# Routing by token block through a table in memory, and a slot of one row tile ahead of the widest expert's slot

## The chip, the cores and the metric

The kernel runs on one core of a Trainium2 chip. The metric is the device time of one execution in microseconds, as the median of several runs. The core has four compute engines that matter here: TensorE (PE, matrix products and transposes; PEld is its weight load), VectorE (DVE), ScalarE (ACT) and GpSimd (POOL). SyncE (SP) issues most of the transfers; GpSimd issues the indirect ones, which gather or scatter rows by a list of indices.

## The reference, cut to what matters

One decoder layer on 1024 tokens of width 1024, all in float32: a mixer (attention and a state-space branch), a cross attention to 256 memory tokens, a mixture of 32 experts with 4 of them per token, and a final norm. The change touches the seam between the cross attention and the experts:

```
h = h + cross_attention(rmsnorm(h), rmsnorm(mem))        # last step: o @ w_o, added to h
xn = rmsnorm(h, norm_moe)
logits = xn @ w_router + b_router                        # (1024, 32)
top_val, top_idx = top_k(logits, 4)
gates = softmax(top_val)
# every expert e gets the list of its tokens, in the order of the tokens:
hb = xn[tokens of e] @ w1[e] + b1[e]                     # 1024 -> 2048
act = clamped swiglu(hb)
h[tokens of e] += gate * (act @ w2[e] + b2[e])           # 1024 -> 1024
out = rmsnorm(h, norm_final)
```

## The kernel before

The kernel has two phases. The first, `phase_abc`, isn't touched. The second, `phase_def`, runs `mixer`, `router` and `experts` one behind the other on each engine's own instruction stream; semaphores order the engines among each other.

**mixer** ends with the output product of the cross attention, the group `XO`: for 8 blocks of 128 tokens and 2 halves of 512 columns, 4 products accumulate in one PSUM bank (the emitting line for all such products is L1247, a helper). VectorE adds each half to `h` (L1353), ScalarE squares and sums `h` (L1493), and GpSimd takes the root (L297 to L299). `moe_row` (L1133) multiplies a block of `h` by its root and by the gain row `g_row` into `xn` or `xnb`, four quarter products a block. Four of the eight blocks are made among the additions and four behind them.

**router** works on all 1024 tokens at once, stage behind stage. SP stores `h` to `acc_dram` (L1559, L1560) and `xn` to `xn_dram` (L1563). TensorE transposes `xn` (L1593), ScalarE and VectorE copy it out as `hT` (L1579, L1634), TensorE makes the logits with the router weights stationary and 512 tokens moving (L1601), and transposes them back (L1607). VectorE finds the top 8 per token (L1649, L1653), makes one-hot rows for the four chosen experts (`m4`, L1662) and their sum `maskE` (L1665). Two products with a triangle and with ones (L1612, L1613) give the rank of each token in its expert's list. VectorE sums counts over blocks (L1675), ranks the experts by their load (L1679 to L1686, result `slot_e`; with this SP asks for the first 12 weight pieces, L1573) and splits the rank into a low part of 7 bits and a high part (L1694 to L1699). The lists come from one-hot products: for 32 pairs of a block and a choice, VectorE makes `lo`, `hi` with the token and `hi` with the gate (L1707 to L1709) and TensorE multiplies them into one bank (L1616). From this bank come the token list, the gate list and, by another product (L1620), the indices of quarter rows `idx_q` (L1719).

**experts** works through slots. `RANK_WIDTH` gives each rank in the order of load a width of rows, from 256 for the fullest expert down to 64 for the two emptiest, which share a slot. `SLOTS` is the order of the slots: rank 0 (256 rows) first, the pair (30, 31), then ranks 1, 29, 2, 28 and so on, and at last 16, 15 and 14 with 128 rows each. The weights of an expert are 12 pieces of 1 MB (8 of w1, 4 of w2) in a ring of 14 places; `load_piece` (L1789) on SP waits until the piece that held the place has been used (`piece_used`). A slot goes so: GpSimd copies the slot's indices (`columns`, L2009 to L2014), gathers quarter rows of `xn_dram` (L2023, four gathers for each tile of 128 rows, 32 tokens by 4 quarters each), VectorE transposes them (L2328) into `xT`, TensorE makes the first layer (L2224, 256 instructions), VectorE and ScalarE the activation, TensorE the second layer: by columns for slots wider than 128 (L2239), by rows for slots of up to 128 (L2147, behind a bias product L2179). GpSimd scatters the result by adding to `acc_dram` (L2042). VectorE clears some tiles at the start of this stage (L2310 to L2317); the semaphore `init_f` counts them, and SP, TensorE and GpSimd wait for its eight steps before their first expert work. Behind the last slot `fin` is read back, normed and stored.

Of the kernel before, what the change touches and what calls it, by code (L numbers as in the profile page):

```python
# [16 lines left out]
F32 = mybir.dt.float32  # L17
# [32 lines left out]
SLOTS = ((0,), (30, 31)) + tuple((r,) for i in range(1, 14) for r in (i, 30 - i)) + ((16,), (15,), (14,))  # L50
# [47 lines left out]
def memory(nc, ctx):  # L98
# [110 lines left out]
    at("br", 201.9375, [E, 1])  # L209
    at("logitT", 194, [E, S])  # L210
    at("logit", 162, [P, NB, E])
    at("top8", 163.5, [P, NB, 8])
    at("idx8", 164, [P, NB, 8], U32)
    at("idxf", 164.5, [P, NB, 8])
    at("gates", 165, [P, NB, 8])
    at("gsum", 165.5, [P, 2, NB])
    at("m4", 165.75, [P, NB, TOPK, E])
    at("maskE", 170, [P, NB, E])
    at("rank", 171, [P, NB, E])
    at("pref", 172, [P, NB + 1, E])  # L220
    at("tri", 173.5, [P, P])
    at("iota_e", 174, [P, E])
    at("iota_w", 174.5, [P, WIN])
    at("dest", 175.5, [P, 4, NB * TOPK])
    at("desti", 176.25, [P, 2, NB * TOPK], I32)
    at("tok1", 176.75, [P, NB])
    at("dumpid", 177, [P, WIN])
    at("lo", 178, [P, 4, P])
    at("hi", 180, [P, 4, 2, WIN])
    at("list_f", 198, [P, 2, WIN])  # L230
    at("list_t", 200, [P, 2, WIN])
# [7 lines left out]
    at("idx_g", 49, [P, WIN], I32)  # L239
# [24 lines left out]
    at("g_row", 0, [P, D])  # L264
# [861 lines left out]
def moe_row(nc, m, b):  # L1126
# [4 lines left out]
    for q in range(4):  # L1131
        out = (m.xn, m.xnb)[b // 4][:, b % 4, WIN * q:WIN * q + WIN].rearrange("p (k r) -> p k r", r=32)
        last = nc.vector.scalar_tensor_tensor(out=out, in0=part(m.h[:, b], q), scalar=m.rs[:, b:b + 1], in1=part(m.g_row[:], q), op0=ALU.mult, op1=ALU.mult)  # L1133
# [3 lines left out]
def mixer(nc, m, a, sem, xn3, g_row_in):  # L1137
# [37 lines left out]
    plan("XO", 16, "dve")  # L1175

# [34 lines left out]
    def on_sync(sp):  # L1211
# [18 lines left out]
        sp.wait_ge(filled, at["XQ"] + 8)  # L1230
        sp.dma_start(m.g_row[:], a.norm_moe.rearrange("(a n) -> a n", a=1).to_broadcast([P, D])).then_inc(g_row_in, 16)

    def on_tensor(pe):
# [98 lines left out]
        copied(pe, at[("O", 7)])  # L1332
        pe.wait_ge(wxo_in, 16)
        for b in range(NB):
            for n in range(2):
                product(lambda k: m.oT[:, k, b * P:(b + 1) * P], lambda k: m.wxo[:, k, n * 512:(n + 1) * 512], 512, H_X)

    def on_vector(dve):
# [91 lines left out]
        copied(dve, index("PB", 15))  # L1430
# [1259 lines left out]
```

## Time and profile before

| | us |
|---|---|
| median of 3 runs | 2451.79 |
| lowest and highest run | 2443.67 and 2454.3 |
| the profiled execution, its own time | 2438.7 |
| its span, first to last instruction | 2437.0 |
| output product of the cross attention starts | 718.2 |
| first expert product starts | 877.1 |
| mean granted TensorE clock | 0.978 |

| engine | busy us | share of the span |
|---|---|---|
| TensorE | 2297.0 | 94% |
| VectorE | 675.6 | 28% |
| ScalarE | 302.6 | 12% |
| GpSimd | 542.3 | 22% |

The profile is one execution. Times in a timeline count from the span's start. A row of a timeline merges equal instructions of one line (x128 is their number) and gives when the first began and how long the whole took. The text in brackets is the idle time of the engine ahead of it and what ended it; "issue" is time in which the engine waited for nothing that the profile shows. Shares of busy time are averages over stages with different limits, so the stages have to be read one by one.

### The profile page before, as it was taken

Reading aid. Unit: us, or ns where it says so; the run is one execution under the profiler, and the core shown is the slowest. Engines: PE = TensorE matmul, PEld = TensorE weight load, DVE = VectorE, ACT = ScalarE, POOL = GpSimd, SP = SyncE. Lnnn points to the kernel's source line nnn. Section 1 sums busy time; section 2 is a strip of 40 time slices with the busy share of each in tenths; the row PEclk is TensorE's granted clock in tenths of the full one; section 3 lists DMA queues with packets and bytes.
Section 4 is the critical chain, followed back from the end, with each engine's and each line's share of the span. In section 5 each row is a group of like instructions: output and inputs, shape, how many; then the busy total and the mean of one; then the engine's idle time right before and its main releaser. Section 6 shows DMA issues by size and latency. Waiting matters only on the chain.

```text
span 2437.0 us, 33822 instructions
## 1 busy us (share of the span) xinstructions
PE 2297.0 (94%) x13692; PEld 1765.9 (72%) x13693; DVE 675.6 (28%) x1684; ACT 302.6 (12%) x637; POOL 542.3 (22%) x1123
## 2 busy tenths in 40 slices
PE   7999988989979669999999999999999999999997
PEld 4546545534444257698988989889889899899875
DVE  2131247223154722122222222212222222222213
ACT  3002045112032000000000010000000100100002
POOL 3715885011002030202011120111111211211203
PEclk9999999999999879999999999999999999999998
DMA  8614210720002645988688798888988989989985
GB/s 202 133 46 48 55 30 2 209 87 0 7 3 117 245 142 186 366 286 286 224 278 298 251 300 265 291 281 265 299 285 271 307 282 312 310 294 305 318 301 165
DMA packets 441043, 508.81 MB, mean 209 GB/s; under 512 B 50997, under 2 KB 367765, under 8 KB 440884
## 3 DMA queue, kind: packets, MB, share of 16 engines
q1 hardware_dynamic: 426968, 470.42, 58.9%
q0 software_dynamic: 12624, 35.90, 6.1%
q8 instruction: 109, 1.79, 0.3%
q10 hardware_dynamic: 1292, 0.30, 0.1%
q14 instruction: 50, 0.41, 0.0%
HBM read 470.60 MB, written 38.25 MB: 209 GB/s over the span
## 4 chain that ended last, share of the span: by engine, by line
PE 76%; DVE 3%; issue 1%; ACT 1%; POOL 1%; ACTq 0%; POOLq 0%; DVEq 0%
PE ps L2224 40%; PE ps L2239 11%; PE ps L1247 10%; PE ps L2147 10%; PE ps L1616 1%; PE ps L2126 1%; PE ps L2179 1%; ACT px L1474 1%; PE ps L1261 1%; PE ps L1601 1%; DVE px L1408 0%; DVE negx L1398 0%; POOL rs L298 0%; DVE xnb L1133 0%; PE ps L1254 0%
## 5 line engine op out<-in xcount | busy, mean ns | idle before, releaser
L2224 PE MATMUL ps<-xT,we 128*128 128x128 f32 (+10 forms) x7680 | 981.6, 290 | 23.8 <-issue 23.8
L2224 PEld LDWEIGHTS ps<-xT,we 128*128 128x128 f32 x7680 | 970.1, 191 | 39.2 <-issue 31.9
L2363 DVE TENSOR_SCALAR glu<-ps,b1s 128x128 f32<-128x128 f32 (+10 forms) x240 | 88.9, 370 | 963.9 <-PE ps L2224 951.6
L2239 PE MATMUL ps<-actT,we 128*128 128x160 f32 (+9 forms) x1792 | 261.1, 307 | 0.0
L2023 POOL DMA_INDIRECT xg<-xn_dram,gx x148 | 152.7, 1031 | 474.1 <-DVE xT L2328 434.4
L2239 PEld LDWEIGHTS ps<-actT,we 128*128 128x128 f32 x1792 | 253.8, 190 | 5.6 <-DVE outT L2389 2.0
L2147 PE MATMUL ps<-we,actT 128*128 128x512 f32 (+1 forms) x576 | 238.2, 595 | 0.7 <-ACT actT L2538 0.7
L2514 ACT ACTIVATE sg<-glu 128x256 f32<-128x256 f32 (+10 forms) x122 | 55.0, 451 | 1253.4 <-DVE glu L2363 1196.7
L2042 POOL DMA_INDIRECT acc_dram<-orow,sx x43 | 66.9, 1556 | 605.0 <-ACT orow L2502 426.5
L2147 PEld LDWEIGHTS ps<-we,actT 128*128 128x128 f32 (+1 forms) x576 | 100.4, 184 | 136.6 <-issue 135.7
L806 PE MATMUL ps<-xnT,wa 128*128 128x512 f32 x384 | 167.9, 598 | 7.1 <-DMA wa<-in_w_in 7.1
L806 PEld LDWEIGHTS ps<-xnT,wa 128*128 128x128 f32 x384 | 73.4, 192 | 99.2 <-issue 91.3
L2389 DVE TENSOR_SCALAR outT<-ps,b2s 128x160 f32<-128x160 f32 (+9 forms) x112 | 44.0, 393 | 175.3 <-PE ps L2239 174.7
L2364 DVE TENSOR_SCALAR lin<-ps,b1s 128x128 f32<-128x128 f32 (+10 forms) x240 | 86.8, 361 | 0.1
L297 POOL TENSOR_SCALAR ss<-ss 128x1 f32<-128x1 f32 (+1 forms) x37 | 10.5, 283 | 268.0 <-ACTq L1494 160.3
L1115 POOL TENSOR_TENSOR scan_t<-V,a 128x128 f32<-128x128 f32 x128 | 58.8, 459 | 30.6 <-DVE V L699 20.6
L1247 PE MATMUL ps<-wo_b,ybT 128*128 128x512 f32 x128 | 57.0, 606 | 9.0 <-DVE ybT L1371 9.0
L2009 POOL COPY gx<-idx_q 128x8 int32 x30 | 5.8, 194 | 256.9 <-DMA acc_dram<-orow,sx 166.1
L2373 DVE TENSOR_TENSOR sg<-sg,glu 128x256 f32<-128x256 f32 (+10 forms) x120 | 54.8, 456 | 8.9 <-ACT sg L2514 8.9
L2374 DVE SCALAR_TENSOR_TENSOR actT<-lin,sg 128x256 f32<-128x256 f32 (+10 forms) x120 | 55.7, 464 | 4.1
L1247 PE MATMUL ps<-hT,wxq 128*128 128x512 f32 x128 | 55.2, 593 | 1.4 <-issue 1.4
L1247 PE MATMUL ps<-wxo,oT 128*128 128x512 f32 x128 | 55.2, 593 | 0.8 <-DVE oT L1429 0.8
(360 smaller groups left out, 1829.3 us busy)
## 6 DMA issues: line engine op xcount, KB each, us to landing
we<-in_w SPq DMA_DIRECT2D x384, 1024.0 KB, 7.3
wa<-in_w_in SPq DMA_DIRECT2D x4, 2048.0 KB, 12.5
xrow<-in_x SPq DMA_DIRECT2D x32, 128.0 KB, 6.4
wa<-in_w_xkv SPq DMA_DIRECT2D x2, 2048.0 KB, 9.9
h<-in_x SPq DMA_DIRECT2D x4, 1024.0 KB, 20.2
acc_dram<-h SPq DMA_DIRECT2D x1, 4096.0 KB, 11.5
fin<-acc_dram SPq DMA_DIRECT2D x8, 512.0 KB, 5.1
out<-fin SPq DMA_DIRECT2D x32, 128.0 KB, 2.3
```

The lines of the kernel that those rows point to most:

```text
L806: last = nc.tensor.matmul(p_bank(i)[:, 0:width], weights(k), moving(k), start=(k == 0), stop=(k == KC - 1))
L1115: tt(m.scan_t[:], now.unsqueeze(1).to_broadcast([P, 2, 2, G]), a8, ALU.mult).then_inc(scan_step, 1)
L1247: last = nc.tensor.matmul(out[:, 0:width], weights(k), moving(k), start=(k == 0), stop=(k == kc - 1))
L2023: pool.indirect_dma_start(xg[q % 2][:, b, :], None, xn_quarters, bass.IndirectOffsetOnAxis(m.gx[:, s % 3, half, b:b + 1], 0), bounds_check ...
L2042: pool.indirect_dma_start(a.acc_dram, bass.IndirectOffsetOnAxis(m.sx[0:rows, s % 3, half:half + 1], 0), orow[q % 2][0:rows, :], None, boun ...
L2147: last = nc.tensor.matmul(m.ps[cols, bank, :], moved[:, 4 * half + k, cols], view[:, k, :], start=False, stop=(half == 1 and k == 3), skip ...
L2224: last = nc.tensor.matmul(bank[:, part * WIN:part * WIN + W], view[:, k, (j % 2) * P:(j % 2 + 1) * P], m.xT[:, k, 0:W], start=(k == 0), st ...
L2239: last = nc.tensor.matmul(m.ps[:, 4 + j % 2, 0:W], view[:, k, (j % 2) * P:(j % 2 + 1) * P], m.actT[:, k, 0:W], start=(k == 0), stop=(k == ...
L2363: v.tensor_scalar(m.glu[:, b, i * WIN:i * WIN + C], bank[:, 0:C], m.b1s[:, col, j:j + 1], LIMIT, ALU.add, ALU.min).then_inc(glu_ok, 1)
L2364: v.tensor_scalar(m.lin[:, b, i * WIN:i * WIN + C], bank[:, WIN:WIN + C], m.b1s[:, col, JF + j:JF + j + 1], LIMIT + 1, ALU.add, ALU.min).t ...
L2374: v.scalar_tensor_tensor(out=m.actT[:, 2 * p:2 * p + 2, 0:C], in0=lin, scalar=1.0 - LIMIT, in1=sg, op0=ALU.max, op1=ALU.mult).then_inc(act ...
L2514: nc.scalar.activation(dst, src, ACT.Sigmoid, scale=ALPHA).then_inc(swished, 1)
```

## The change

Four things are done.

1. The router works by token block, between the output products of the cross attention, which move from `mixer` into `router`. TensorE's order is: output product (b, 0), transposes of block b - 1 of `h` (not of `xn`), ranks of block b - 2, output product (b, 1), logits of block b - 1. The logits take the transposed tokens as stationary operand and the router weights, which GpSimd has multiplied by the norm's gain, as the 32 moving columns; VectorE scales them by the root afterwards (`choose`). The ranks are one product with the triangle and one with the running count `cum` and ones, accumulated. `place` turns the rank into the address of a record in a table.
2. The lists come by memory: a record of token and gate (8 bytes) for each token and choice is scattered by GpSimd, 32 indirect transfers of 128 records, to `table_dram` (32768 records, filled beforehand with a dump row's index), and ScalarE's queue reads the whole table back as `list` when all are in. The one-hot products, their operands and the copies behind them are gone.
3. `h` and `xn` are stored block by block; the last block of `xn` by ScalarE's queue. SP asks for the weights as soon as the experts are ranked, and waits for the stores of `xn` ahead of the seventh piece and for those of `h` ahead of the eleventh. The tiles of the expert stage are cleared behind the ranking of the experts instead of behind the lists, and GpSimd gathers the first rows ahead of its other copies and ahead of its wait for `init_f`.
4. The slot of rank 16 (128 rows) comes ahead of the slot of rank 0 (256 rows). It stood third from last.

The core of the diff:

```diff
-SLOTS = ((0,), (30, 31)) + tuple((r,) for i in range(1, 14) for r in (i, 30 - i)) + ((16,), (15,), (14,))
+SLOTS = ((16,), (0,), (30, 31)) + tuple((r,) for i in range(1, 14) for r in (i, 30 - i)) + ((15,), (14,))
...
+    def on_sync(sp):
+        sp.wait_ge(blank_ok, 1)
+        sp.dma_start(a.table_dram.rearrange("(p n) c -> p n c", p=P), m.blank[:].bitcast(F32)).then_inc(table_in, 16)
+        scored_all(sp)
+        sp.dma_start(m.g_row[:], a.norm_moe.rearrange("(a n) -> a n", a=1).to_broadcast([P, D])).then_inc(g_row_in, 16)
         for b in range(NB):
+            copied(sp, at[("XO", b, 1)])
+            sp.dma_start(a.acc_dram[b * P:(b + 1) * P], m.h[:, b]).then_inc(acc_out, 16)
+            if b < WIN // P:
+                sp.dma_start(a.acc_dram[S + b * P:S + (b + 1) * P], m.h[:, b]).then_inc(acc_out, 16)
+            if b:
+                store_xn(sp, b - 1)
         sp.wait_ge(sorted_ok, 1)
...
         for i in range(PRELOADED):
+            if i == 6:
+                rows_stored(sp)
+            if i == 10:
+                sp.wait_ge(acc_out, 16 * (NB + WIN // P))
             load_piece(sp, m, a, 0, i, sp.snap(first, min_val=0, max_val=E - 1))
...
+        store_xn(act, NB - 1)
+        act.wait_ge(table_out, 16 * NB * TOPK)
+        act.dma_start(m.list[:], a.table_dram.rearrange("(p n) c -> p n c", p=P)).then_inc(list_in, 16)
...
+        for b in range(NB):
+            output(b, 0)
+            if b:
+                transposes(b - 1)
+            if b == 2:
+                pe.wait_ge(consts, 2)
+            if b >= 2:
+                ranks(b - 2)
+            output(b, 1)
+            if b == 1:
+                pe.wait_ge(weights_ok, 1)
+            if b:
+                logits(b - 1)
+        transposes(NB - 1)
+        ranks(NB - 2)
+        logits(NB - 1)
+        ranks(NB - 1)
...
+        def place(b):
+            ready(dve, "RK", b)
+            read(v.tensor_tensor(m.m4[:, b], m.m4[:, b], bank("RK", b)[:, 0:E].unsqueeze(1).to_broadcast([P, TOPK, E]), ALU.mult))
+            copied(dve, at[("RK", b)])
+            ch.link(v.reduce_sum(m.rank[:, b, :], m.m4[:, b], AX.X))
+            rank, low, high, first = (m.ranki[:, i, b, :] for i in range(4))
+            ch.link(v.tensor_copy(rank, m.rank[:, b, :]))
+            ch.step(v.tensor_scalar(low, rank, P - 1, 8, ALU.bitwise_and, ALU.logical_shift_left))
+            ch.link(v.tensor_scalar(high, rank, 7, None, ALU.logical_shift_right))
+            ch.link(v.tensor_tensor(low, low, high, ALU.bitwise_or))
+            v.tensor_tensor(m.place[:, b, :], low, first, ALU.bitwise_or).then_inc(placed, 1)
...
+        for b in range(NB):
+            add(b, 0)
+            if b:
+                transposed(b - 1)
...
+            if b >= 2:
+                place(b - 2)
+            add(b, 1)
+            if b:
+                choose(b - 1)
+                rows(b - 1)
+        transposed(NB - 1)
+        place(NB - 2)
+        dve.wait_ge(rooted, NB)
+        rows(NB - 1, range(2))
+        choose(NB - 1)
+        rows(NB - 1, range(2, 4))
+        place(NB - 1)
...
+        dve.wait_ge(table_in, 16)
+        begin_experts()
+        dve.wait_ge(list_in, 16)
+        token = m.list[:].bitcast(I32)[:, :, 0]
+        v.tensor_copy(m.tokf[:], token.rearrange("p (e w) -> p e w", w=NB)[:, :, 0:2]).then_inc(listed, 1)
+        ready(dve, "QI")
...
+        def scatter(b):
+            pool.wait_ge(placed, 2 * b + 2)
+            for k in range(TOPK):
+                pool.indirect_dma_start(a.table_dram, bass.IndirectOffsetOnAxis(m.place[:, b, k:k + 1], 0), m.rec[:, b, k, :], None,
+                                        bounds_check=last_place, oob_is_err=True).then_inc(table_out, 16)
+        for b in range(NB):
+            pool.wait_ge(squared, b + 1)
+            root(nc, m, ch, b, D).then_inc(rooted, 1)
+            if b >= 2:
+                scatter(b - 2)
+        scatter(NB - 2)
+        scatter(NB - 1)
+        rows_stored(pool)
...
+        def first_rows():
+            gather(0)
+            pool.wait_ge(init_f, 8)
+
+        indexed(pool)
+        columns(0, first_rows)
         columns(1)
```

`choose(b)` scales the logits and adds the bias, takes the top 8 and their indices, the differences to the greatest (ScalarE makes the exps), the one-hot rows, their sum `maskE` and the running count: nine small operations. `rows(b)` is `moe_row`.

## Rows read from the trace of the kernel before

**Rows 1.** The page's groups (engine, operation, count, busy us, mean ns, idle before).

```profile
L2224 PE MATMUL ps<-xT,we 128*128 128x128 f32 (+10 forms) x7680 | 981.6, 290 | 23.8 <-issue 23.8
...
L2023 POOL DMA_INDIRECT xg<-xn_dram,gx x148 | 152.7, 1031 | 474.1 <-DVE xT L2328 434.4
...
L2042 POOL DMA_INDIRECT acc_dram<-orow,sx x43 | 66.9, 1556 | 605.0 <-ACT orow L2502 426.5
```

**Rows 2.** The chain of work that ended last, 650 to 960 us: start, us, what.

```profile
718.19 55.22 PE ps L1247 x128
...
820.33 29.70 PE ps L1616 x64
...
853.38 0.68 DVE idx_q L1719
...
861.36 15.78 issue
877.14 58.04 PE ps L2224 x256
```

**Rows 3.** TensorE's timeline: start, us, engine, line, operation, count.

```profile
782.09 3.88 PE L1593 MATMUL ps<-ident,xnb 128*128 128x128 f32 x32 [0.90 <-DVE xnb L1133]
...
852.24 1.11 PE L1620 MATMUL ps<-list_t,spread 128*128 128x64 f32 x8 [2.22 <-DVE idx_g L1717]
...
2288.52 28.75 PE L2224 MATMUL ps<-xT,we 128*128 128x128 f32 x256
...
2405.40 14.00 PE L2147 MATMUL ps<-we,actT 128*128 128x512 f32 x32
```

**Rows 4.** What SP's queue waited for, 870 to 2437 us: total, times, longest.

```profile
SPq L1789 <- PE ps L2224: 799.8, 112, 15.5
```

**Rows 5.** VectorE's timeline, 770 to 900 us.

```profile
773.43 0.69 DVE L1353 TENSOR_TENSOR h<-h,ps 128x512 f32<-128x512 f32 x1 [2.75 <-PE ps L1247]
774.03 1.67 DVE L1133 SCALAR_TENSOR_TENSOR xn<-h,rs,g_row 128x256 f32<-128x256 f32 x4
...
781.96 4.87 DVE L1634 COPY hT<-ps 128x512 f32<-128x512 f32 x8
...
813.12 0.18 DVE L1679 SCALAR_TENSOR_TENSOR key<-pref,rev 1x32 f32<-1x32 f32 x1
...
818.03 0.18 DVE L1694 CAST desti<-dest 128x32 int32<-128x32 f32 x1
818.25 0.18 DVE L1695 TENSOR_SCALAR desti<-desti 128x32 int32<-128x32 int32 x1
```

**Rows 6.** GpSimd's timeline, 770 to 900 us.

```profile
778.75 3.76 POOL L1738 COPY spread<-ident 128x512 f32<-128x512 f32 x1
...
863.56 1.32 POOL L2023 DMA_INDIRECT xg<-xn_dram,gx  x1 [0.19 <-issue]
...
866.49 1.00 POOL L2023 DMA_INDIRECT xg<-xn_dram,gx  x1 [0.30 <-issue]
867.80 1.00 POOL L2023 DMA_INDIRECT xg<-xn_dram,gx  x1 [0.30 <-issue]
```

**Rows 7.** The timeline of all engines, 855 to 884 us.

```profile
870.80 1.25 DVE L2328 STREAM_TRANSPOSE xT<-xg 128x1024 f32<-128x1024 f32 x1 [6.84 <-DMA xg<-xn_dram,gx]
```

**Rows 8.** SP's timeline.

```profile
816.22 26.98 SPq L1789 DMA_DIRECT2D we<-in_w  x12
```

**Rows 9.** Transfers by issue: count, KB each, median us from issue to landing.

```profile
we<-in_w SPq DMA_DIRECT2D x384, 1024.0 KB, 7.3
...
acc_dram<-orow,sx POOLq DMA_INDIRECT x45, 6.9
...
kp_dram<-Krow SPq DMA_DIRECT2D x1, 256.0 KB, 4.3
```

**Rows 10.** Busy time by window: TensorE, its loads, VectorE, ScalarE, GpSimd; clock, DMA share, GB/s.

```profile
690.00:718.00 28.00, 20.95 (x88) 12.85 (x88) 18.66 (x33) 12.03 (x37) 0.00 (x0) 1.00 0.00 1
845.00:850.00 5.00, 5.00 (x12) 1.90 (x10) 2.55 (x9) 0.00 (x0) 0.00 (x0) 1.00 1.09 384
```

More of the change, by code:

```diff
@@ L208, in memory @@
     at("wr", 206, [P, KC, E])
[L209 to L231, printed above, removed]
+    at("br", 207, [P, E])
+    at("rec", 207.25, [P, NB, TOPK, 2])
+    at("place", 207.5, [P, NB, TOPK], I32)
+    at("hB", 130, [P, 4, KC, P])
+    at("m4", 146, [P, NB, TOPK, E])
+    at("logit", 150, [P, NB, E])
+    at("maskE", 151, [P, NB, E])
+    at("cum", 152, [P, NB + 1, E])
+    at("tri", 153.5, [P, P])
+    at("iota_e", 154, [P, E])
+    at("top8", 154.25, [P, NB, 8])
+    at("idx8", 154.5, [P, NB, 8], U32)
+    at("idxf", 154.75, [P, NB, 8])
+    at("gates", 155, [P, NB, TOPK])
+    at("gsum", 155.25, [P, 2, NB])
+    at("rank", 155.5, [P, NB, TOPK])
+    at("ranki", 155.75, [P, 4, NB, TOPK], I32)
+    at("tokf", 158, [P, E, 2])
+    at("blank", 199, [P, E * NB, 2], I32)
+    at("list", 186, [P, E * NB, 2])
     at("widths", 48, [P, E])
@@ L263, in memory @@
     at("qcol_i", 55.71875, [P, 1], I32)
-    at("g_row", 0, [P, D])
+    at("g_row", 80, [P, D])
+    at("dumpid", 55.75, [P, 1])
     at("spread", 52, [P, 4, P])
@@ L1625, in on_vector @@
+    def on_vector(dve, begin_experts):
         ch = Chain(dve, step_dve)
         v = nc.vector
[L1628 to L1636 removed]
@@ L1676, in on_vector, with read, add, transposed @@
-        ch.link(v.tensor_tensor(m.rank[:].rearrange("p b e -> p (b e)"), bank(RK)[:, 0:NB * E],
-                                m.pref[:, 0:NB, :].rearrange("p b e -> p (b e)"), ALU.add))
+        def read(ins):
+            ins.then_inc(r_dve, 1)
+        def add(b, n):
+            ready(dve, "XO", b, n)
+            out = m.h[:, b, n * 512:(n + 1) * 512]
+            read(v.tensor_tensor(out, out, bank("XO", b, n), ALU.add))
+        def transposed(b):
+            ready(dve, "RT", b, 1)
+            read(v.tensor_copy(m.hB[:, b % 4, 4:8, :].rearrange("p k t -> p (k t)"), bank("RT", b, 1)))
@@ L1678, in on_vector @@
+        transposed(NB - 1)
+        place(NB - 2)
[4 more added lines that the diff above has]
+        place(NB - 1)
+        ready(dve, "TOT")
         key = (m.key[:, 0], m.key[:, 1])
-        ch.link(v.scalar_tensor_tensor(out=key[0], in0=m.pref[0:1, NB, :], scalar=float(E), in1=m.rev[:], op0=ALU.mult, op1=ALU.add))
+        read(v.scalar_tensor_tensor(out=key[0], in0=bank("TOT")[0:1, 0:E], scalar=float(E), in1=m.rev[:], op0=ALU.mult, op1=ALU.add))
@@ new lines, in on_vector @@
+        begin_experts()
[3 more added lines that the diff above has]
+        ready(dve, "QI")
+        read(v.tensor_scalar(m.idx_q[:].rearrange("p e w b -> p b e w"), bank("QI")[:, 0:4 * 2 * E].rearrange("p (b e w) -> p b e w", b=4, w=2),
+                             4.0, m.qcol[:, 0:1], ALU.mult, ALU.add))
+        copied(dve, at[("QI",)])
+        dve.sem_inc(idx_q_ok, 1)
@@ L1980, in on_gpsimd, with columns @@
         regs = [pool.alloc_register(f"expert_pool{i}") for i in range(4)]
-        def columns(s):
+        def columns(s, now=None):
             experts = []
```

404 lines of the change are left out of this document (189 added, 215 removed).

## The prediction

> **What bounds the kernel now.** I read the page's costliest groups first, then the chain of work that ended last between 718 and 878 us, then each engine's timeline there, then SP's waits. From 877.14 us to the last expert product, which ends at 2405.40 + 14.00 = 2419.4 us, TensorE runs without a gap worth the name: the first-layer products (L2224) sat idle 23.8 us in all, once, before their first instruction [rows 1]. The expert stage is therefore TensorE's own 1542.3 us. It isn't waiting for weights: the queue that loads them is the one that waits, 799.8 us on L2224 alone [rows 4], because the ring of 14 pieces is full. Behind the experts come 17.6 us of final norm and stores.
>
> So only what lies ahead of 877.14 us can change the time, unless the change makes the experts starve. There the chain goes from the output product of the memory attention (718.19 us, 55.2 us long) over the token-block softmax, ranks and one-hot products (L1616, 29.7 us) to the quarter indices idx_q (853.38 us), then 15.78 us of "issue" in which TensorE waits for the first gathered rows [rows 2]. From the end of the output product (773.4) to the first expert product (877.1) 103.7 us pass in which TensorE does little but small router products. The change attacks this stretch.
>
> **The change, part by part.** A is the moment when the new interleaved stage on TensorE has ended the logits of block 6, the last thing it does behind the last output product.
>
> 1. TensorE, 718.2 us to A. The output products stay: 55.2 us. Between them go 7 x 8 transposes of h at 0.12 to 0.14 us (L1593: 3.88/32; L1620: 1.11/8), 1.05 us a block, 7.4 us; 6 rank pairs (four instructions of 128x32, 0.139 us each by L1620), 0.55 us, 3.3 us; 7 logit groups of 16 instructions, each with 128x128 weights and 32 moving columns. The trace doesn't show that form; it lies between 28.75/256 = 0.112 us (128 columns, L2224) and 1.11/8 = 0.139 us (64 columns, L1620) [rows 3], 1.8 to 2.2 us a block, and I take 2.1, 14.7 us in all. Sum 80.6 us, so 798.8; with 1.2 us for waits between groups A = 800, bounds 797 and 806. A block costs TensorE 10.6 us. VectorE has to do in it two additions of 0.69 (L1353), a copy of 0.6 (L1634: 4.87/8), about 20 small dependent steps at the pitch of 0.22 us that L1694 and L1695 show (818.03 to 818.25), and four row products at 0.42 (L1133: 1.67/4): 8.1 us [rows 5]. GpSimd has a root of three small instructions, which I put at 1.5 us, and four record scatters; nothing shows an 8-byte scatter, the nearest rows are the gathers, 1.31 us apart (866.49 to 867.80), and the accumulating scatters at 1.56 us each [rows 1, 6], so 6.7 to 7.7 us a block. TensorE sets the pace in this stage, and the others hide behind it.
>
> 2. A to the record of block 7. VectorE: choose(6) and rows(6), 2.3 + 1.6; copy 0.7; TensorE logits(7) 2.0 meanwhile beside place(6) 2.3; two row products 0.8; choose(7) 2.2; two more row products 0.8; place(7) with the gate 2.2. Sum 12.9: A + 12.9. Behind it the ranking of experts, from 813.12 [rows 5] to just before the first request for weights, 2.6 us, with the same operations: sorted at A + 15.5 = 815.5. The weights are asked for at 816.2 us now [rows 8]: they don't start earlier. The memsets of the expert stage, which stood between idx_q and 861.36 [rows 2], some 6 us, now follow the sort. They are hidden by the landing of the table: they end at A + 22, and the list isn't there before A + 24; without that cover they would cost up to 6 us.
>
> 3. The list. Four scatters of block 7 start at A + 13.0, the last at A + 16.9. The landing of the last: before, the fourth gather starts at 867.80 and VectorE takes the rows at 870.80, 3.0 us; with full queues an accumulating scatter takes 6.9 us [rows 6, 7, 9]. The list is one load of 256 KB: 4.3 us like the quiet store of kp_dram, up to the 7.3 us of a 1 MB weight piece [rows 9], since the weights are in flight by then (before, 12 pieces kept the queues at 384 GB/s until about 850) [rows 10]. Then a cast 0.2, the quarter product 1.1, idx_q 0.7.
>
> 4. The first gather. In the old kernel the chain from idx_q to TensorE was 23 us: seven further VectorE steps and memsets, 5 copies, 8 gathers (256 rows), 2 transposes. Now: one copy, about 1.5 us, four gathers, 3.9 us to the start of the last, 3.0 (quiet) to 6.9 us (queues full) to land, transpose 1.25 and a hand-over, 1.3 [rows 6, 7]. The slot of 128 rows spares four gathers at 1.31 = 5.2 us; the order of the 30 others is the same and the sum of TensorE's work is the same 1542.3 us.
>
> Sum from A: 16.9 + 3.0 + 0.2 + 4.3 + 2.0 + 1.5 + 3.9 + 3.0 + 1.3 = 36.1 us if all is quiet (0.2 for the hand-over to ScalarE), 16.9 + 6.9 + 0.2 + 7.3 + 2.0 + 1.5 + 3.9 + 6.9 + 1.3 = 46.9 if the queues are full. The weights start at the very moment of the last scatters, so I take a value nearer the upper end, 43. TensorE's first expert product: 800 + 43 = 843 us, between 833 and 853. Before 877.1: **34 us gained**, bounds 24 and 44. What the restart from idle costs TensorE is inside the 58.04 us of the first layer of the old first slot [rows 2]; it idles before the new one too, so that stays.
>
> 5. Does the earlier start starve the experts? 12 pieces took some 33 us (816.2 to about 850 at 384 GB/s) [rows 8, 10], 2.7 us a piece. A slot of 128 uses its 12 pieces in 28.75 + 14.0 + 1.1 = 43.6 us, 3.6 us a piece [rows 3], and it starts 27 us behind the first request. Cover: 27 us where it was 61. Pieces 12 and 13 leave SP behind ten small loads at about 850 and are wanted at 887; the bias rows of the pair are now asked for among the pieces of the second slot, more than 80 us ahead of their use. Nothing waits; if loading ran at 5.2 us a piece, half the measured rate, the last pieces of the slot would just begin to be late.
>
> The blank table (256 KB) and g_row are loaded while SP is idle; the stores of h and xn, 9 MB, move from behind the product into the 80 us of it, where the queues are empty. The weight pieces wait for them only from the seventh on; the last store of xn leaves at A + 10.7 and needs some 5 us.
>
> A rule that speaks against the change: GpSimd writes the descriptors of the records while VectorE is some 75% busy. What the trace has of the two together: a copy of 128x512 on GpSimd took 3.76 us while VectorE ran row products, and the first gather 1.32 where the later ones took 1.00 [rows 6]. The Trainium skill, SBUF — State Buffer ("SBUF: two separate sides" and "Who interferes with whom"), says that a VectorE instruction in a two-port mode, or one with two SBUF inputs against GpSimd's reads, shuts GpSimd out of a shared port pair for its whole length. By that rule the scatters would stretch; the rows above fit it. It is the mechanism of rival 1.
>
> **Rivals.**
> 1. GpSimd becomes the bound (slower). The 32 record scatters come from about 745 us on, with 10 us of roots among them (six and a bit at 1.5); the last must be out at 816.9 for my forecast. If each costs c, they end at 755 + 32c. At c = 1.31 GpSimd waits for VectorE; beyond 1.9 it sets the end, and from c = 3.0 us the 34 us are gone (755 + 96 = 851). At the 3.76 us of that copy they end at 875, 58 us late: a gain of 34 becomes a loss of 24 us, 2476 on the scale of the median. For: rows 6, and VectorE is busier than in any stretch where gathers run now. Against: 148 gathers beside VectorE's expert work have a mean of 1.03 us [rows 1].
> 2. Everything behind the last scatter waits in full queues (the upper ends of 3 and 4, and somewhat more, as the first 12 pieces are all queued at once): TensorE starts at 853 or later, gain 20 to 24 us, 2430.
> 3. The earlier start does starve the first two slots: 10 us lost, gain 24, 2428. For: cover falls from 61 to 27 us. Against: rates above.
> 4. The change doesn't do what it says: the interleaved stage is as much longer as the router is shorter. VectorE's 8.1 us a block would have to become 14.9, or the clock would have to fall to half in the stage for some 34 us; against it the stretch of 690 to 718 us, where TensorE is 75% busy in small pieces at a granted clock of 1.00 [rows 10]. About no change, 2450.
>
> **How the numbers follow.** Forecast (parts 1 to 5) 0.68, rival 1 0.07 (slower) and 0.04 as a half-way backlog near no change, rival 2 0.11, rival 3 0.04, rival 4 0.06 (most of it near no change, 0.02 slower). The profiled execution took 2438.7 us (span 2437.0), 13 us below the median of the three runs, 2451.8. Gained 34 us: the profiled one would be 2404.7, the median 2417.5; I give the median. The bounds 44 and 24 give 2408 and 2428; rival 2 and a spread of 10 us between runs of the same kernel stretch that to 2403 to 2436. 0.5% is 12 us, about what a measurement tells from no change: faster 0.83, same 0.08, slower 0.09.
>
> **What would show it.** In the profile after: the output products end near 800 us, TensorE with hardly a gap from 718 to there; the weights' first request within 3 us of 816; the record scatters at 1.3 us each (beyond 1.9: rival 1); last scatter start to list landed 8 to 14 us; first expert product near 843 us on a slot of 128 rows; from there 1542 us to the last product, with no waits of TensorE for pieces (else rival 3). What would make the prediction wrong is above all the price of the 8-byte scatters, which no row shows.

## The result, and the profile after

| | before | after |
|---|---|---|
| median, us | 2450.8 (4 runs, 2443.7 to 2454.3) | 2411.35 (4 runs, 2406.1 to 2414.9) |
| ratio, with its 95% interval | | 0.9841 [0.9812, 0.9870] |
| profiled execution's own time | 2438.7 | 2411.0 |
| its span | 2437.0 | 2409.0 |
| output product starts | 718.2 | 728.8 |
| first expert product starts | 877.1 | 848.5 |
| last expert product ends | 2419.4 | 2390.1 |
| mean granted TensorE clock | 0.978 | 0.975 |

The kernel is 1.6% faster: 39.4 us by these medians (35.1 when both were measured again, 2445.08 and 2409.98). The forecast was 2417.5 us, in a range of 2403 to 2436. The two profiled executions differ by only 28 us, since that of before was its most favourable one, 12 us under the median, and that of after stood at its median. What the change did is therefore read from the stretch between the first output product and the first expert product, which hardly differs between executions of the same kernel: 158.95 us before (158.92 in a second profile of it) and 119.68 after (119.71 in a second).

The page's groups after, columns as in [rows 1], and what SP's queue waited for, as in [rows 4]:

```profile
L2317 PE MATMUL ps<-xT,we 128*128 128x128 f32 (+10 forms) x7680 | 980.9, 290 | 13.3 <-issue 13.3
...
L2113 POOL DMA_INDIRECT xg<-xn_dram,gx x148 | 153.7, 1038 | 482.5 <-DVE xT L2425 442.4
```

```profile
SPq L1877 <- PE ps L2317: 769.9, 110, 12.7
```

The work of the experts is unchanged: 980.9 us where it was 981.6, and the queue of weights still waits for TensorE. The chain of waits through the new stage (start, us, what), which answers to [rows 2]:

```profile
728.83 10.57 PE ps L1616 x24
739.40 0.87 PE ps L1627 x8
740.27 3.44 PE ps L1616 x8
743.71 1.71 PE ps L1637 x16
745.41 3.52 PE ps L1616 x8
748.92 0.87 PE ps L1627 x8
...
806.95 1.09 POOL table_dram L1821
...
817.06 1.16 issue
...
822.29 5.55 DMA table_dram<-rec,place
827.86 5.16 DMA list<-table_dram
...
835.29 0.68 DVE idx_q L1783
836.82 11.70 issue
848.51 21.51 PE ps L2317 x174
```

First TensorE alone: output products (L1616), transposes (L1627) and logits (L1637) in turn, a new transpose group every 10 us, without a gap. Then from 806.95 on GpSimd's record scatters (L1821) are the chain, then two landings, then gathers. TensorE's timeline at the end of the interleaved stage shows its last logits for block 6; its next instruction starts at 805.10, the moment A:

```profile
799.88 3.68 PE L1616 MATMUL ps<-wxo,oT 128*128 128x512 f32 x8
803.40 1.87 PE L1637 MATMUL ps<-wr,hB 128*128 128x32 f32 x16
805.10 1.07 PE L1627 MATMUL ps<-ident,h 128*128 128x128 f32 x8
```

GpSimd's timeline from there on answers to [rows 6]:

```profile
816.04 1.02 POOL L1821 DMA_INDIRECT table_dram<-rec,place  x1 [0.30 <-issue]
818.46 0.97 POOL L1821 DMA_INDIRECT table_dram<-rec,place  x1 [1.39 <-DVE place L1726]
...
822.29 0.97 POOL L1821 DMA_INDIRECT table_dram<-rec,place  x1 [0.30 <-issue]
...
841.77 0.99 POOL L2113 DMA_INDIRECT xg<-xn_dram,gx  x1 [0.30 <-issue]
```

The eight scatters of blocks 5 and 6 run back to back, 1.28 us apart (the first two 1.39 and 1.32); GpSimd then stands idle 1.39 us for the places of block 7. SP asks for the weights at 821.10, in the middle of the last scatters:

```profile
821.10 25.47 SPq L1877 DMA_DIRECT2D we<-in_w  x12
```

Busy time by window, columns as in [rows 10]: the interleaved stage, the tail of the router, the experts.

```profile
728.00:806.00 78.00, 77.22 (x329) 46.15 (x328) 46.60 (x169) 15.16 (x35) 29.60 (x60) 1.00 0.27 107
806.00:849.00 43.00, 8.34 (x38) 7.66 (x37) 22.28 (x78) 2.36 (x6) 22.15 (x31) 0.52 0.75 265
849.00:2390.00 1541.00, 1540.31 (x10484) 1359.84 (x10482) 361.00 (x898) 119.43 (x228) 249.52 (x341) 1.00 0.86 284
```

TensorE is busy 77.2 of 78 us in the first and 1540.3 of 1541 in the last. All of the new kernel's idle time at this seam lies in the 43 us between.

### The profile page after: what moved, and what is told of

Same layout as the page of the kernel before. It is cut to its first block, busy times and chain, and to the rows that moved or that the text cites. A ratio compares the mean times of both kernels' runs of the same rounds, so it can differ in the third digit from the quotient of the medians.

```text
span 2409.0 us, 34021 instructions
## 1 busy us (share of the span) xinstructions
PE 2278.1 (95%) x13746; PEld 1772.3 (74%) x13747; DVE 661.9 (27%) x1677; ACT 304.8 (13%) x652; POOL 571.9 (24%) x1157
## 4 chain that ended last, share of the span: by engine, by line
PE 76%; DVE 1%; issue 1%; ACT 1%; POOL 1%; DMA 0%; ACTq 0%; POOLq 0%; DVEq 0%
PE ps L2317 40%; PE ps L2332 11%; PE ps L2240 10%; PE ps L1240 8%; PE ps L1616 2%; PE ps L2219 1%; PE ps L2272 1%; ACT px L1450 1%; PE ps L1254 1%; PE ps L1637 0%; POOL table_dram L1821 0%; DVE px L1395 0%; POOL rs L295 0%; DVE negx L1385 0%; PE ps L1247 0%
## 5 line engine op out<-in xcount | busy, mean ns | idle before, releaser
L2317 PE MATMUL ps<-xT,we 128*128 128x128 f32 (+10 forms) x7680 | 980.9, 290 | 13.3 <-issue 13.3
L2113 POOL DMA_INDIRECT xg<-xn_dram,gx x148 | 153.7, 1038 | 482.5 <-DVE xT L2425 442.4
L1616 PE MATMUL ps<-wxo,oT 128*128 128x512 f32 x128 | 58.3, 601 | 0.8 <-DVE oT L1416 0.8
L1240 PEld LDWEIGHTS ps<-wo_b,ybT 128*128 128x128 f32 x128 | 25.2, 199 | 41.4 <-issue 31.6
L1240 PE MATMUL ps<-wo_a,yaT 128*128 128x512 f32 x128 | 55.2, 593 | 0.0
## 6 DMA issues: line engine op xcount, KB each, us to landing
wa<-in_w_in SPq DMA_DIRECT2D x4, 2048.0 KB, 12.5
```

The source lines that it names most:

```text
L1240: last = nc.tensor.matmul(out[:, 0:width], weights(k), moving(k), start=(k == 0), stop=(k == kc - 1))
L1616: last = nc.tensor.matmul(out, m.oT[:, k, b * P:(b + 1) * P], m.wxo[:, k, n * 512:(n + 1) * 512], start=(k == 0), stop=(k == H_X - 1))
L2113: pool.indirect_dma_start(xg[q % 2][:, b, :], None, xn_quarters, bass.IndirectOffsetOnAxis(m.gx[:, s % 3, half, b:b + 1], 0), bounds_check ...
L2317: last = nc.tensor.matmul(bank[:, part * WIN:part * WIN + W], view[:, k, (j % 2) * P:(j % 2 + 1) * P], m.xT[:, k, 0:W], start=(k == 0), st ...
```

## The experiments

The theory: the gain is the router's work hidden between the output products (some 34 us) plus the four gathers that the narrow first slot spares (some 5 us); GpSimd keeps up, and the price behind the last scatter is landings in queues that the weights fill. The rivals are those of the prediction. Below, **the seam** is the time from the first output product to the first expert product, in the profile of each kernel. A ratio stands as it was recorded, from runs of both kernels in one session, and isn't the quotient of the two medians beside it (after, again: 0.9856).

| kernel | median, us | its before, us | ratio, 95% interval | seam, us |
|---|---|---|---|---|
| before, again | 2442.67 (1 run) | 2443.91 | | 158.92 |
| slot order alone | 2440.29 | 2445.08 | 0.9975 [0.9964, 0.9986] | 153.47 |
| after, again | 2409.98 | 2445.08 | 0.9845 [0.9819, 0.9872] | 119.71 |
| after with the old slot order | 2417.27 | 2445.08 | 0.9882 [0.9853, 0.9911] | 124.87 |
| records scattered twice | 2433.14 | 2445.08 | 0.9944 [0.9923, 0.9965] | 140.91 |
| weights behind the list | 2398.87 | 2443.91 | 0.9821 [0.9806, 0.9836] | 113.75 |
| shorter tail | 2405.22 | 2443.91 | 0.9835 [0.9820, 0.9850] | 115.52 |
| shorter tail, weights behind | 2402.36 | 2443.91 | 0.9823 [0.9809, 0.9836] | 112.60 |
| before with early clears | 2448.58 | 2446.31 | 1.0008 [0.9999, 1.0018] | 158.90 |
| clears later | 2408.52 | 2446.31 | 0.9843 [0.9830, 0.9857] | 119.87 |
| clears later, weights behind | 2400.80 | 2446.31 | 0.9814 [0.9800, 0.9828] | 113.48 |
| all three | 2400.75 | 2446.31 | 0.9810 [0.9797, 0.9823] | 112.59 |

**The two parts apart.** The kernel after, run again:

> The changed kernel once more, for a second profile and a second ratio. In its first profile the output product starts at 728.8 us where the profile of before has 718.2, though the code ahead of it differs in nothing that matters; from there to the first expert product it takes 119.7 us where before took 158.9, 39.2 less. Theory (the 10.6 us ahead of the output product are spread between executions, from short stretches at half clock): the start of the output product lies elsewhere this time, between 716 and 730, and the 119.7 us return within 1 us; ratio 0.982 to 0.987. Rival (something in the change costs 10 us ahead of the output product): it starts at 728 to 730 again, and does so in each kernel that has the new router.

The seam came back within 0.03 us, and the output product started at 728.74 us, 0.1 us from the first profile: what the rival of this expectation said, though inside the theory's range too.

The slot order, put alone into the kernel before, and taken back out of the kernel after:

```
 kernel before:
-SLOTS = ((0,), (30, 31)) + ... + ((16,), (15,), (14,))
+SLOTS = ((16,), (0,), (30, 31)) + ... + ((15,), (14,))
```

> The kernel before, with nothing changed but the order of the slots (the 128-row slot of rank 16 first). The first gather is four transfers at 1.3 us in place of eight, and one transpose stands ahead of the first product in place of two. Theory: the first expert product comes 5.0 us earlier (the second transpose started 5.0 us behind the first), so 2446 against 2451, ratio 0.998. Rival (the narrow first slot uses up its pieces before the ring is refilled): no gain or a loss of some us, with waits of TensorE for weights in the first two slots.

> The changed kernel with the old order of slots (256 rows first). Theory: eight gathers and two transposes again, 5.2 us for the issues, and somewhat more for landing while the weights fill the queues: the first expert product comes 5 to 7 us later than in the changed kernel, ratio to before 0.986. Rival (the order is only there to avoid starving): the same start, and TensorE would not wait either; then within 1 us of the changed kernel.

The seam became 5.4 us shorter by the order alone (158.92 to 153.47) and 5.2 us longer without it (119.71 to 124.87), and the medians moved by 4.8 and 7.3 us. In the chain of the kernel with the order alone, the wait for the rows before a first product of 128 columns is 10.3 us:

```profile
856.14 0.68 DVE idx_q L1719
...
864.12 10.32 issue
874.44 9.19 PE ps L2224 x64
```

So of the seam's 39.3 us some 5.3 are the slot and 34 the rest of the change, and the two parts add up. The 34 aren't all router work hidden between products: from the end of `idx_q` to the first expert product the kernel with the order alone takes 17.6 us (856.82 to 874.44) and the kernel after 12.5 (835.97 to 848.51), since the clears and most of GpSimd's copies no longer stand there. These 5 us belong to part 3 of the change; no run takes them apart from the router.

**Twice the scatters**, against rival 1 (GpSimd the bound). Each record goes also to a second table that nobody reads, and the reading of the list waits for all 64 transfers:

```
 for k in range(TOPK):
     pool.indirect_dma_start(a.table_dram, ... m.rec[:, b, k, :], ...)
+    pool.indirect_dma_start(a.table2_dram, ... m.rec[:, b, k, :], ...)
```

> The changed kernel with each record scattered twice, the second time to another table that nobody reads: 64 indirect transfers of 128 records instead of 32. This doubles the price c of a record scatter, 1.28 us in the trace after, to 2.56. Theory (by the formula of rival 1, GpSimd sets the end from 1.9 us on): GpSimd needs 8 x 1.28 + 1.4 = 11.7 us a block where TensorE needs 10.0, the backlog adds up, the last scatter goes out about 22 us later than at 822.3, and the kernel takes 20 to 24 us more than the changed one, about 2433. Rival (what counts behind the last block is only the landing and the queues): the last record goes out at most 10 us later (eight more in the last two blocks) and the kernel takes 5 to 10 us more, about 2419.

GpSimd's timeline at the end of the 64 scatters:

```profile
846.09 0.97 POOL L1821 DMA_INDIRECT table_dram<-rec,place  x1 [0.30 <-issue]
847.36 0.97 POOL L1823 DMA_INDIRECT table_dram<-rec,place  x1 [0.30 <-issue]
```

Now they run from 758.3 on with nothing but the roots and one pause of 1.3 us between them, still at 1.28 us, and the seam grew by 21.2 us. The last starts 117.3 us behind the first output product. The rival's formula, 755 + 32c against an output product at 718.2, gives 118.4 us for a pair at 2.55. So the rival's mechanism exists, where the prediction put it, and by the same formula it would have begun to cost at 1.9 us a scatter. But the 21.2 us aren't all GpSimd's. VectorE stands idle for 23.3 us in seven waits that the profile puts down to another core or an unknown queue and that the kernel after doesn't have. One of them stands between two steps of the ranking of the experts, which depend on VectorE alone:

```profile
843.73 0.18 DVE L1771 MAX8 ranked<-key 1x8 f32<-1x32 f32 x1 [2.60 <-remote]
```

Through these waits VectorE's clears end so late that the list, asked for at 849.51, is read only at 855.9; with the 2.7 us that its landing takes in the next experiment it could have been read 3.7 us earlier. So at least 3.7 of the 21.2 us are VectorE's, and what holds it stays open. The last scatter starts 23.9 us later in the seam, less than the price of the 32 added ones (41 us), since in the kernel after GpSimd is busy for only 29.6 of the 78 us of the stage.

**The weights behind the list**, against rival 2 (full queues):

```
 sp.wait_ge(sorted_ok, 1)
+sp.wait_ge(list_in, 16)
 first = sp.alloc_register("expert_first")
```

Together with it ran one more profile of the kernel before, to see how much its own stages shift: its seam was 158.92 us again, its output product started at 723.0 where the first profile has 718.2.

> The kernel before, for a second profile. In all four profiles of kernels with the new router the output product of the cross attention starts at 727.6 to 730.0 us; in the two with the old router at 718.2 and 721.0. Theory (spread between executions: both profiles of the old router fell on favourable ones, 5 to 12 us below the median of their runs): this one has its own time near the median of 2445, and the output product starts at 723 to 730. Rival (the new router costs 8 to 10 us ahead of the output product, always): it starts at 718 to 721 again, and the own time is near 2438 again.

> The changed kernel, in which SP asks for the first weights only when the list has been read back. Theory (the record scatters and the list land late because the weights fill the queues): the last scatter takes 3 to 4 us from its start to its landing instead of 5.5, the list 4.0 to 4.5 instead of 5.2, so the first expert product comes 2 to 3 us earlier than in the changed kernel, and TensorE still doesn't wait for weights, although the first piece is asked for only some 16 us ahead of its use: about 2408 where the changed one has 2410. Rival A (landing is the cost of the scatter itself): same start, no gain. Rival B (starving, rival 3 of the prediction): TensorE waits for pieces in the first slot, 5 us or more lost.

The chain:

```profile
816.32 2.12 DMA table_dram<-rec,place
818.47 2.74 DMA list<-table_dram
821.23 0.21 DVE tokf L1782
...
829.97 5.28 DMA xg<-xn_dram,gx
835.28 1.26 DVE xT L2426
836.62 30.17 PE ps L2318 x256
```

Two landings shrink: the records' from 5.55 to 2.12 us and the list's from 5.16 to 2.74; the gathers', which still have the weights before them, stays at 5.3 (5.4). Sum 5.9 us, the whole of the seam's change and twice the 2 to 3 us expected. Nothing is paid back for it: the expert products take 1541.1 us from the first to the last, where the kernel after has 1541.6. The weights are asked for at 821.99, 14.6 us ahead of the first expert product, and the only row of TensorE's waits from 860 to 2380 us (what it waited for: total, times, longest) is the one that the kernel after has too:

```profile
PE ps L2241 <- ACT actT L2636: 0.7, 1, 0.7
```

**A shorter tail.** Behind the last output products VectorE makes the places before the normed rows, and GpSimd scatters block b-2 before it makes the root of block b:

```
                 choose(b - 1)
-                rows(b - 1)
+                if b < NB - 1:
+                    rows(b - 1)
         transposed(NB - 1)
         place(NB - 2)
-        dve.wait_ge(rooted, NB)
-        rows(NB - 1, range(2))
+        rows(NB - 2)
         choose(NB - 1)
-        rows(NB - 1, range(2, 4))
         place(NB - 1)
+        rows(NB - 1)
 ...
-            pool.wait_ge(squared, b + 1)
-            root(nc, m, ch, b, D).then_inc(rooted, 1)
             if b >= 2:
                 scatter(b - 2)
+            pool.wait_ge(squared, b + 1)
+            root(nc, m, ch, b, D).then_inc(rooted, 1)
```

> The changed kernel with two reorderings behind the last output product: VectorE makes the rows of blocks 6 and 7 where it would otherwise wait or behind place(7), and GpSimd scatters the records of block b - 2 ahead of the root of block b instead of behind it. Theory (the last record is held by VectorE's order, and by scatters of blocks 5 and 6 that GpSimd still has before it): the first scatter of block 7 goes out at about 815 instead of 818.5 (on the scale where the output product starts at 728.8), the first expert product 3 to 4 us earlier, about 2406 to 2407. Rival (something else holds the end: the store of the last rows, which now leaves later, or the memsets): less than 1 us gained, or a loss.

> Both edits together: if they are independent, 5 to 7 us less than the changed kernel, 2403 to 2405, ratio to before 0.982. If the later stores of the last rows come to stand in the way of the list, only 3 to 4 us.

Alone it makes the seam 4.2 us shorter, but not where it was meant to: the last scatter starts 91.6 us behind the first output product where it was 93.5, 1.9 us; the rest is the records' landing, 2.4 us in place of 5.5, because the weights are now asked for behind the last scatter (826.48 against 825.84), less 0.8 us by which the list landed later. With the weights behind the list only 1.2 us are left of it (113.75 to 112.60), because the clears of VectorE, which hid behind the landing, are now the last thing before the list is read:

```profile
816.24 0.91 DVE xg L2406
...
819.88 0.91 DVE brow L2411
820.95 0.91 DVE crow L2412
821.97 1.99 PE ps L1677 x8
```

That is the cover of which the prediction said that its loss costs up to 6 us. By the landing in the kernel with the weights behind alone (2.76 us from the list's issue, which is at 818.33 here) the list could have been read at 821.1; it was read at 821.8.

**The clears on GpSimd.** The prediction had nothing for the 10.6 us by which the output product starts later in the profile after. They fall into three parts. 4.6 us lie ahead of the first product with `wo_b` (half of the mixer's output weights), which comes before everything that the change touches: it starts between 544.7 and 549.7 us in the three profiles with the old router and no early clears, and between 546.2 and 554.4 in the seven with the new router and early clears. These ranges overlap, so this part is most likely spread between executions. 2.6 us lie between there and the first product with `wxq` (query weights of the cross attention): the same three profiles take 67.83 to 67.94 us for it and the seven 70.24 to 70.61. And 3.4 us lie between the first product with `kmT` (keys of the memory) and the output product. The trace shows one cause in the first of the two stretches. In the kernel after, GpSimd's first clears (L1794 to L1797) follow the last root of the second norm at once, and the last of VectorE's eight norm products (L1365) takes 1.86 us instead of about 0.75:

```profile
612.65 1.86 DVE L1365 TENSOR_SCALAR xnb<-h,rs 128x1024 f32<-128x1024 f32 x1 [1.21 <-POOL rs L296]
```

```profile
612.54 0.96 POOL L1794 MEMSET xg<- 128x1024 f32 x1
613.43 0.54 POOL L1796 MEMSET blank<- 128x512 int32 x1
```

TensorE's transposes wait for it. Four kernels test this: early clears put into the kernel before, clears made later in the kernel after, and the latter together with the other edits.

```
 kernel before, behind the last root of the second norm:
+        nc.gpsimd.memset(m.xg0[:], 0.0)
+        ch.link(nc.gpsimd.memset(m.list_t[:, 0], 0.0))
+        nc.gpsimd.iota(m.list_t[:, 0], [[1, WIN]], ...)
         pool.wait_ge(xn_ready, NB)

 kernel after, ahead of the first clear (through a helper, here written out):
+        pool.wait_ge(filled, at["XQ"] + 1)
         g.memset(m.xg0[:], 0.0)
```

> The kernel before, with the first clears of the new GpSimd order (the 128x1024 clear of the first slot's rows, and a clear and an iota of one row of 256 values) put behind the last root of the mixer's second norm, where the new kernel has them; nothing waits for them. Theory C (the clears run beside VectorE's last norm product, which then takes 1.9 us in place of 0.76, TensorE gets its transposes late, stretches them and loses clock in the stage after): from the first product with wo_b to the first wxq product 70.5 us in place of 67.9, from the first product with kmT to the first output product 50 to 53 in place of 49.5, and the time 2.5 to 6 us over the kernel before. Theory S (the new kernels' later output product is spread between executions): both stretches as in the kernel before, 67.9 and 49.5, and the time within 2 us of it.

> The kernel after, with GpSimd waiting until the last transposed rows of h stand in SBUF before its first clear. Theory C: the norm product is back at 0.76 us, wo_b to wxq back at 67.9 us (from 70.5), kmT to output product back at 49.5 (from 53), so the output product starts 3 to 6 us earlier after the first product with wo_b; the router's part stays at 119.7 us from output product to first expert product; median 2405 to 2408, a ratio of 0.982 to 0.983 where the kernel after had 0.9845. Theory S: stretches unchanged at 70.5 and 53, and the ratio as the kernel after. If the clears delay something behind them now (the triangle and the iota for the places): the same stage of 119.7 grows, by up to 2 us.

> The last one, and SP waits for the list in SBUF before it asks for the next pieces of weights. Output product to first expert product 113.8 us, as with that wait alone; the two stretches ahead of it 67.9 and 49.5 (theory C) or 70.5 and 50.4 to 53 (theory S). Both gains in full: median 2396 +- 4, ratio 0.979 to 0.981, against 0.9821 with the wait alone.

> The shorter tail of VectorE and GpSimd, the weights behind the list, and the clears later, all in the kernel after. Output product to first expert product 112.6 us, stretches ahead 67.9 and 49.5 (theory C) or 70.3 and 50.4 (theory S); median 2395 +- 4, ratio 0.978 to 0.981. The clears of the later slots end nearer the list here: if they hold the list's reading they cost up to 2 us, and this one is then no faster than the one without the shorter tail.

The last norm product in the kernel before with early clears, then in the kernel after with later ones:

```profile
613.26 1.65 DVE L1378 TENSOR_SCALAR xnb<-h,rs 128x1024 f32<-128x1024 f32 x1 [1.20 <-POOL rs L299]
```

```profile
612.18 0.75 DVE L1365 TENSOR_SCALAR xnb<-h,rs 128x1024 f32<-128x1024 f32 x1 [1.21 <-POOL rs L296]
```

So it is shown that the early clears stretch this product, by 0.9 to 1.1 us, both when they are added and when they are taken away; it is so in all eight profiles with early clears and in none of the six without. They aren't all of the first stretch. With early clears in the kernel before it became 68.75 us (not the 70.5 expected), with later clears 68.0 us in two kernels but 69.5 in the third, with all edits. The first 32 products with `wo_b`, more than 40 us ahead of the clears, account for the rest; here they are in the kernels before and after and in the one with all three edits:

```profile
544.73 15.51 PE L1247 MATMUL ps<-wo_b,ybT 128*128 128x512 f32 x32 [8.95 <-DVE ybT L1371]
```

```profile
549.33 17.01 PE L1240 MATMUL ps<-wo_b,ybT 128*128 128x512 f32 x32 [8.95 <-DVE ybT L1358]
```

```profile
549.71 17.06 PE L1240 MATMUL ps<-wo_b,ybT 128*128 128x512 f32 x32 [8.95 <-DVE ybT L1358]
```

In the 8 us from their start the granted clock was 0.81 in the kernel before and 0.62 and 0.61 in the other two. So the 2.6 us of the kernel after are 1.5 here and 1.1 at the clears. Four of the other kernels with early clears lose little here (15.5 to 15.7 us); in them the transposes behind the stretched product take 5.6 us in place of 3.9.

What lengthens the second stretch is the granted clock too. From the first `kmT` product to the output product, in the profile of before and then of after (columns as in [rows 10]):

```profile
668.67:718.19 49.52, 36.54 (x160) 24.09 (x160) 32.31 (x56) 22.86 (x72) 0.00 (x0) 1.00 0.03 12
```

```profile
675.87:728.83 52.96, 40.69 (x161) 26.93 (x161) 32.51 (x56) 22.84 (x72) 0.62 (x3) 0.90 0.03 11
```

The mean is 1.00 and the stretch 49.5 us in five profiles: before, before again, the slot order alone, and the two of clears later without the shorter tail. In the nine others it is 0.90 to 0.97, with 50.4 to 53.4 us. These nine are all eight kernels' profiles with early clears and one of the six without, that with all three edits. So the lower clock goes with the early clears wherever they are, but it also came once without them; what makes it fall stays open. In the medians nothing of it can be told: 1.0008 with the early clears, whose interval ends at 1.0018 (4.4 us), under the middle of the 2.5 to 6 us expected; and 0.9843 with the later ones, where the kernel after has 0.9845 and 0.9841 and 0.982 to 0.983 was expected.

The four kernels with the weights behind the list have medians from 2398.9 to 2402.4 us and ratios from 0.9810 to 0.9823; the five without (after, after again, shorter tail, clears later and, for its order, 5 us off, the old slot order) lie above. The pair that shows it best was measured in one session, clears later without and with the wait: 0.9843 and 0.9814, with intervals that don't meet. With the shorter tail the step is only 0.9835 to 0.9823, inside the intervals. That wait is worth 0.2 to 0.3% to the kernel after; which of the four is best can't be told.

## Why the prediction was right

**What bounds the kernel.** Right. The expert stage took 1541.6 us where 1542.3 were taken over from before, and behind it came 18.9 us (17.6). The whole difference stands ahead of it.

**The interleaved stage.** A block took 9.97 us, not 10.6. From the first output product to A: 76.3 us, where 81.8 were worked out. The term that was too large is that of the logits, 1.71 us in place of 2.1 (7 x 0.39 = 2.7 us); the form with 32 moving columns costs 0.107 us, under the lower bound of 0.112. It is the largest of the mis-sized terms, and 2.1 was taken near the upper bound of 2.2 without a reason given. Transposes cost 0.87 instead of 1.05 (1.3 us), the ranks 0.36 instead of 0.55 (1.1 us), and the 1.2 us for waits between groups didn't come; the 16 groups of output products at 3.52 us (3.45 before) cost 1.1 us more. VectorE (46.6 of 78 us busy) and GpSimd (29.6) hid behind TensorE, as written.

**A to the last scatter.** Predicted 16.9, measured 17.2 us. The places of block 7 stood at A + 13.1 (predicted 12.9). GpSimd was closer to the bound than the text had it: it made eight scatters back to back here and had 1.4 us to spare.

**The price of the record scatter**, named as the most likely cause of an error: 1.28 us from start to start, taken at 1.31. It is the pitch of the gathers [rows 6], the nearer of the two rows given. The stretching beside a busy VectorE that rival 1 drew from the 3.76 us copy doesn't occur for these scatters: 0.97 to 1.09 us each but for the first two (1.2 and 1.3), with VectorE 60% busy. The gathers of the expert stage stayed at 1038 ns (1031).

**The list and the first gather.** Predicted 43 us from A, between 36.1 and 46.9; measured 43.4. Its terms: 17.2 to the last scatter, 5.6 landing (bounds 3.0 and 6.9), 5.2 for the list (4.3 and 7.3), 2.9 for cast, quarter product and `idx_q` (2.0), 1.8 to the first gather (1.5), 4.0 (3.9), 5.4 landing (3.0 and 6.9), 1.3. The reason given for a value near the upper end, that the weights start with the last scatters, holds: with the weights behind the list the two landings ahead of them fall to 2.1 and 2.7 us, below both lower bounds.

**The sum.** 34 us were predicted and the seam gained 39.3: 5.5 from the interleaved stage, less 0.4 from A on. The first expert product came at 848.5 and not at 843 only because the output product began 10.6 us later, about which the prediction had said nothing. It took all that lies ahead of 718 us as unchanged. That step failed in the profile. What the runs show in its place is only in part an effect of the change: 1.1 us from GpSimd's clears, which were moved to right behind the last roots; 4.9 us from stretches at a lower granted clock (1.5 and 3.4), whose cause is open; and 4.6 us ahead of both, most likely spread. Two sums of the text are a little off and change nothing: 28.75 + 14.0 + 1.1 is 43.85 and not 43.6 us, and 2451.8 less 34 is 2417.8.

**The median.** 2417.5 was predicted and 2411.35 measured, and the seam's gain was 5 us larger than forecast. The medians alone can't confirm the 34 us more closely than some 5 us: they gave 39.4 the first time and 35.1 the second. **The rivals.** 1: not at this price; at twice the price the seam grew by 21 us, of which at most some 17.5 are GpSimd's. 2: in part; 5.9 us, inside the bounds. 3: didn't occur, even with a cover of 14.6 us in place of 27. 4: didn't occur; the granted clock was 1.00 through the stage.

## What to carry to other kernels

Work that is small on the bounding engine can be hidden block by block between large products, and its price can be summed from the nearest forms in the trace; what stays exposed is the tail behind the last product, so read that one instruction by instruction, with the landing of each dependent transfer. Small transfers on which the next stage hangs should leave before the bulk load that follows them: asking for the weights behind the list, 7 us later in the seam (99.1 us behind the first output product in place of 92.3), made it 5.9 us shorter and cost nothing, because the first use lay 14.6 us off. And of every instruction that a change moves earlier, ask what it now runs beside, also where no queue or semaphore connects them.

## What the runs showed of the hardware

- 128 scattered records of 8 bytes (one indirect transfer) cost GpSimd 1.28 us from start to start: with VectorE 60% busy in the kernel after (728 to 806 us), and with VectorE 33% busy at the end of the 64 scatters (5.9 of 18 us, 830 to 848). The landing took 2.1 us in quiet queues and 5.5 us behind the first pieces of weights.
- Clears on GpSimd stretched a product of 128x1024 float32 on VectorE, which ran beside them, from 0.75 us to 1.65 (early clears in the kernel before) and 1.86 (kernel after). In both kernels the first clear had started 0.11 us ahead of the product and ran 0.85 us beside it, and the product ended 0.55 us behind the end of a second, smaller clear. The Trainium skill, SBUF — State Buffer ("Who interferes with whom"), says that a `tensor_scalar` can enter a mode that uses the port pair shared with GpSimd, and that who issues first keeps the other out for its whole instruction. With the first clear alone that would give, as an estimate, 0.85 + 0.75 = 1.6 us here; the trace agrees in direction, and nearly in size (1.65 and 1.86). The prediction had weighed this rule only with GpSimd as the loser.
- Sixteen products with 128x128 weights and 32 moving columns cost 0.107 us each at full clock, little less than those with 128 columns (0.112 us) [rows 3].
